# Gate and shift rows of a transformer kernel: spread by products with the identity, or by DRAM and back

## The reference, cut to what matters

```python
def ada_modulation(c, w, b):
    mod = jax.nn.silu(c) @ w + b
    return jnp.split(mod[:, None, :], 6, axis=-1)

# even layer
x = x + g_m * mix                                  # mix: two kinds of attention, then w_out
h = rms_norm(x, norm_ffn) * (1 + sc_f) + sh_f
return x + g_f * swiglu_2(h, ffn_gate, ffn_up, ffn_down)

# odd layer
x = x + g_m * (o.reshape(B, S, -1) @ w_out)        # o: sparse attention
h = rms_norm(x, norm_ffn) * (1 + sc_f) + sh_f
return x + g_f * moe_swiglu(h, router_w, router_b, exp_gate, exp_up, exp_down)
```

## Time and profile before

| | us |
|---|---|
| median of 3 runs | 2050.56 |
| lowest, highest | 2047.79, 2051.41 |
| the profiled execution | 2053.22 |
| its span, first to last instruction | 2051.3 |
| PE busy in the span | 1926.4 (94%) |
| DVE busy | 1370.7 (67%) |
| ACT busy | 1012.5 (49%) |
| POOL busy | 79.2 (4%) |

### The profile page before, as it was taken

How to read it: one execution, slowest core, us unless ns; L and a number is a source line. 1 busy time by engine, 2 the same in 40 slices (tenths; PEclk the granted TensorE clock), 3 DMA queues, 4 the chain that set the end, 5 groups by cost and what they waited for, 6 DMA issues and landing times.

```text
span 2051.3 us, 24825 instructions
## 1 busy us (share of the span) xinstructions
PE 1926.4 (94%) x9656; PEld 1614.3 (79%) x9656; DVE 1370.7 (67%) x1963; ACT 1012.5 (49%) x1372; POOL 79.2 (4%) x96
## 2 busy tenths in 40 slices
PE   8999899989998899998988999896879999999997
PEld 6888788878887778886876878795758888778886
DVE  6776776677666647676465844658574546588888
ACT  6434444454345544345445334434544435577776
POOL 1000000000000000000000100000010000000001
PEclk9999999999999999999998999998989999999998
DMA  9877477667762347775332785332075757699995
GB/s 322 267 241 235 160 250 245 226 199 247 242 233 72 111 164 232 241 245 165 84 102 82 264 296 190 122 93 93 11 265 182 246 158 250 204 351 379 379 380 211
DMA packets 270971, 432.85 MB, mean 211 GB/s; under 512 B 11075, under 2 KB 201862, under 8 KB 270598
## 3 DMA queue, kind: packets, MB, share of 16 engines
q1 hardware_dynamic: 250832, 356.65, 52.2%
q0 software_dynamic: 17968, 67.55, 9.7%
q10 hardware_dynamic: 2054, 7.06, 0.9%
HBM read 422.83 MB, written 14.68 MB: 213 GB/s over the span
## 4 chain that ended last, share of the span: by engine, by line
PE 82%; DVE 8%; ACT 6%; issue 2%; DMA 2%; ACTq 0%; DVEq 0%; SPq 0%
PE acc L2192 11%; PE acc L2194 10%; PE acc L2193 10%; PE gate_bank L2192 7%; PE gate_bank L2194 7%; PE gate_bank L2193 7%; PE up_bank L2192 7%; PE up_bank L2193 7%; PE up_bank L2194 7%; DVE w_low L1414 3%; ACT w_high L835 2%; ACT probs L950 1%; PE turn_bank L2326 1%; DMA raw<-in_e_ffn_up 1%; PE misc_bank L2261 1%
## 5 line engine op out<-in xcount | busy, mean ns | idle before, releaser
L1414 DVE TENSOR_TENSOR w_low<-raw,w_high 128x2048 fp32r<-128x2048 f32 (+2 forms) x370 | 772.7, 2099 | 299.6 <-ACT w_high L835 296.6
L835 ACT CAST w_high<-raw 128x2048 fp32r<-128x2048 f32 (+2 forms) x370 | 647.3, 1756 | 358.2 <-PE up_bank L2194 191.8
L2192 PE MATMUL gate_bank<-w_high,u_parts 128*128 128x512 f32 (+2 forms) x516 | 205.5, 398 | 14.6 <-DVE u_parts L1436 5.6
L2194 PE MATMUL gate_bank<-w_high,u_parts 128*128 128x512 f32 (+2 forms) x516 | 199.9, 387 | 0.0
L2193 PE MATMUL gate_bank<-w_low,u_parts 128*128 128x512 f32 (+2 forms) x516 | 199.9, 387 | 0.0
L2192 PE MATMUL up_bank<-w_high,u_parts 128*128 128x512 f32 (+2 forms) x500 | 194.7, 389 | 0.0
L2193 PE MATMUL up_bank<-w_low,u_parts 128*128 128x512 f32 (+2 forms) x500 | 194.3, 389 | 0.0
L2194 PE MATMUL up_bank<-w_high,u_parts 128*128 128x512 f32 (+2 forms) x500 | 194.2, 388 | 0.0
L2192 PE MATMUL acc<-w_high,hidden_high 128*128 128x512 f32 x476 | 189.5, 398 | 1.5 <-DVE w_low L1414 0.8
L2194 PE MATMUL acc<-w_high,hidden_low 128*128 128x512 f32 x476 | 186.8, 392 | 0.0
L2193 PE MATMUL acc<-w_low,hidden_high 128*128 128x512 f32 x476 | 186.2, 391 | 0.0
(11 more groups left out here) (515 smaller groups left out, 3376.5 us busy)
## 6 DMA issues: line engine op xcount, KB each, us to landing
raw<-in_o_exp_down SPq DMA_DIRECT2D x40, 1024.0 KB, 7.1
raw_ada<-in_e_ada_w POOLq DMA_DIRECT2D x24, 1024.0 KB, 5.9
raw_ada<-in_o_ada_w POOLq DMA_DIRECT2D x24, 1024.0 KB, 5.8
raw<-in_ffn_pre_wg SPq DMA_DIRECT2D x44, 512.0 KB, 5.8
raw<-in_ffn_pre_wu SPq DMA_DIRECT2D x44, 512.0 KB, 7.1
raw<-in_ffn_pre_wd SPq DMA_DIRECT2D x22, 1024.0 KB, 7.6
raw<-in_ffn_post_wg SPq DMA_DIRECT2D x44, 512.0 KB, 4.5
raw<-in_ffn_post_wu SPq DMA_DIRECT2D x44, 512.0 KB, 5.7
```

The source lines that it names most:

```text
L835: ins = nc.scalar.copy(dst(WH[c % RING]), src(RAW[RAW_SLOT[c]]))
L1414: ins = nc.vector.tensor_tensor(dst(WL[c % RING]), src(RAW[RAW_SLOT[c]]), dst(WH[c % RING]).bitcast(F32), ALU.subtract)
L2192: nc.tensor.matmul(to, sh, mh, start=first, stop=False, **kw)
L2194: return nc.tensor.matmul(to, sl, mh, start=False, stop=last, **kw)
```

## The change

Each of the six vectors is written by POOL from its eight columns to a row of a new DRAM tensor `GATES` (1024 runs of one number, `gate_out`) and read back into all 128 partitions (`gate_back`, 512 KiB). All six calls of `gate_row` on PE, ACT's copies, and their semaphores, are gone; DVE waits for `gate_in[k]` instead. Writes 0 and 1 stand in `ffn3` (after chunk 35), read 0 after chunk 37, read 1 in the even attention; writes 2 to 5 and reads 2 to 4 in `ffn4`, after chunk 47 and ahead of the late constants and the zeros; read 5 in the odd attention. The scale of the experts' norm gets a tile of its own, `ADA_LAST`, made in tile 6 of `ffn4`; `scale_of(N_OFFN)` goes.

```diff
+        ADA_LAST = sb("ada_scale_of_experts", [P, DC])
+        GATES = nc.dram_tensor("gate_rows", [6, D], F32, kind="Internal").ap()
...
+            def gate_out(k, columns):
+                pool.dma_start(GATES[k, :].rearrange("(c p) -> p c", p=P), columns, allow_slow_non_contiguous=True).then_inc(gates_out, 16)
+
+            def gate_back(k, row):
+                pool.dma_start(row, GATES[k:k + 1, :].broadcast_to([P, D])).then_inc(gate_in[k], 16)
...
             for q in range(2, ADA_DONE[3] + 1):
                 ada(q)
+                if q == ADA_DONE[2] + 3:
+                    pool.wait_ge(ada_read, 24)
+                    gate_out(0, MOD[:, 16:24])
+                    gate_out(1, MOD[:, 40:48])
+                if q == ADA_DONE[2] + 5:
+                    pool.wait_ge(gates_out, 32)
+                    pool.wait_ge(x_ready, 4 * X_POOL + 4)
+                    gate_back(0, ROWS[0][:, :])
...
+            pool.wait_ge(x_ready, 4 * X_FINAL1 + 4)
+            pool.wait_ge(at_max, GH * (G_FOX + 1))
+            gate_back(1, ROWS[1][:, :])
             for q in range(ADA_DONE[3] + 1, 48):
                 ada(q)
+            pool.wait_ge(ada_summed, 48)
+            pool.wait_ge(ada_read, 48)
+            pool.wait_ge(ada_ready, 1)
+            gate_out(2, MOD[:, 64:72])
+            gate_out(3, ADA_LAST[:, :])
+            gate_out(4, MOD[:, 72:80])
+            gate_out(5, MOD[:, 88:96])
+            pool.wait_ge(gates_out, 96)
+            pool.wait_ge(x_ready, 4 * X_EWO + 4)
+            for k, to in ((2, ROWS[0][:, :]), (3, AROW), (4, BROW)):
+                gate_back(k, to)
             pool.wait_ge(at_max, GH * (G_WIN + 2))
...
+            pool.wait_ge(x_ready, 4 * X_FFN4 + 4)
+            pool.wait_ge(at_max, GH * (G_DSA + 1))
+            gate_back(5, ROWS[1][:, :])
             pool.wait_ge(x_ready, 4 * X_OWO + 4)
             row(0, a["final_norm_2"].unsqueeze(0))
...
-            gate_row(0, X_POOL)
             blocks(b + 3, 3)
             square_sum(N_EFFN, 0)
-            gate_row(1, X_FINAL1)
             square_sum(N_EFFN, 1)
...
-            gate_row(2, X_EWO)
             prep(b + 3)
-            gathered_row(3, AROW, (GB, UB))
             square_sum(N_OFFN, 0)
-            gathered_row(4, BROW, (MB, SB))
             square_sum(N_OFFN, 1)
...
-            act.wait_ge(x_ready, 4 * X_FFN4 + 4)
-            gathered_row(5, ROWS[1], (GB, UB))
...
-                                dve.wait_ge(row_done, row + 1)
+                                dve.wait_ge(gate_in[row], 16)
...
+            def last_scale(i):
+                if i == 6:
+                    dve.wait_ge(ada_read, 48)
+                    nc.vector.scalar_tensor_tensor(ADA_LAST[:, :], MOD[:, 80:88], 1.0, vec("o_ffn"), ALU.add, ALU.mult
+                                                   ).then_inc(ada_ready, 1)
+
+            ffn(4 * FB, "ffn4", FFN_TILES, None, ada_chunk(4), last_scale)
...
-            scale_of(N_OFFN, U_OFFN, vec("o_ffn"), MOD[:, 80:88])
-            dve.sem_inc(ada_ready, 1)
...
-            dve.wait_ge(row_done, 5)
+            dve.wait_ge(gate_in[3], 16)
+            dve.wait_ge(gate_in[4], 16)
...
-            gate_row(0, MOD[:, 16:24])
             even_down(2)
             even_down(3)
-            gate_row(1, MOD[:, 40:48])
             turn_rows(N_EFFN)
-            pe.wait_ge(row_done, 2)
...
-            gate_row(2, MOD[:, 64:72])
             odd_down(2)
             odd_down(3)
-            pe.wait_ge(ada_read, 48)
-            pe.wait_ge(ada_ready, 1)
-            gate_row(3, ADA)
-            gate_row(3, MOD[:, 72:80], (MB, SB))
-            gate_row(4, MOD[:, 88:96])
             turn_rows(N_OFFN)
...
-            pe.wait_ge(row_done, 6)
```

More of the change, by code:

```diff
@@ L514, in two_blocks_kernel @@
         vec_turned, vec_ready, c_ready = sem("vec_turned"), sem("vec_ready"), sem("c_ready")
-        row_in, row_mm, row_done = sem("row_in"), sem("row_mm"), sem("row_done")
+        row_in, gates_out, gate_in = sem("row_in"), sem("gates_out"), [sem(f"gate_in{k}") for k in range(6)]
         dve_chain = sem("dve_chain")
@@ L885, in high_modulated @@
                     nc.scalar.copy(UH[:, first:first + 2, :], T[:, first:first + 2, :]).then_inc(u_hi, 2)
[L887 to L892, removed]
             def ffn(m0, name, tiles, n=None, at_tile=None):
@@ L1277, in _ @@
                     ins = nc.scalar.activation(T[:, c, :], ACC[:, c * S:(c + 1) * S], ACT.Identity,
-                                               bias=MOD[:, 72 + c:73 + c], scale=ADA[:, c:c + 1])
+                                               bias=MOD[:, 72 + c:73 + c], scale=ADA_LAST[:, c:c + 1])
                 ins.then_inc(t_act, 1)
             rows_high_part(1)
-            act.wait_ge(x_ready, 4 * X_FFN4 + 4)
-            gathered_row(5, ROWS[1], (GB, UB))
             b0 = STREAM["moe"]
@@ L1767, in scale_of @@
                 dve.wait_ge(u_hi, DC * u)
-                dve.wait_ge(ada_read, 48 if n == N_OFFN else ADA_DONE[3])
+                dve.wait_ge(ada_read, 48 if n == N_OMIX else ADA_DONE[3])
                 chain.link(nc.vector.scalar_tensor_tensor(ADA[:, :], scale, 1.0, gain, ALU.add, ALU.mult))
@@ L1861, in _ @@
             norm_modulated(N_EFFN, U_EFFN, vec("e_ffn"), MOD[:, 32:40], MOD[:, 24:32], (b + 5, b + 6))
-            ffn(4 * FB, "ffn4", FFN_TILES, None, ada_chunk(4))
+            def last_scale(i):
[4 more added lines that the diff above has]
+            ffn(4 * FB, "ffn4", FFN_TILES, None, ada_chunk(4), last_scale)
             update(A_FFN4, STREAM["ffn4"] + 3 * FB - 1, row=1)
@@ L1948, in _ @@
                 for c in (2 * cp, 2 * cp + 1):
-                    ins = nc.vector.tensor_scalar(T[:, c, :], ACC[:, c * S:(c + 1) * S], ADA[:, c:c + 1],
+                    ins = nc.vector.tensor_scalar(T[:, c, :], ACC[:, c * S:(c + 1) * S], ADA_LAST[:, c:c + 1],
                                                   MOD[:, 72 + c:73 + c], ALU.mult, ALU.add)
@@ L2068, in weighed_row @@
             def weighed_row(t):
-                dve.wait_ge(row_done, 6)
+                dve.wait_ge(gate_in[5], 16)
                 dve.wait_ge(y_second, t + 1)
@@ L2263, in modulation @@
                 mm.then_inc(ada_used, 1)
[L2265 to L2271, removed]
             def ffn(m0, name, tiles, u, chunk=lambda i: None, turned_second=None, amid_first=None):
```

## The result

| | before | after |
|---|---|---|
| median, runs | 2050.34 (5) | 2063.06 (5) |
| lowest, highest | 2046.88, 2051.41 | 2060.07, 2066.52 |
| the profiled execution, its span | 2053.22, 2051.3 | 2063.77, 2061.6 |

The account below looks back on a forecast made before the run. PE, 82% of the chain that ended last, was taken to bound the kernel. Gains of 5.2 and 7.2 us at the projections less 2.0 for the zeros gave 10.4 off 2050.6: 2040.2 us, range 2033 to 2046.5.

Parts of the forecast that it names:

- The products removed: Both output projections without row products and copies: 5.2 us gained at the even one, 7.2 at the odd one.
- Amid `ewo`: Even output projection: first row's products and a wait behind block 2 go, so block 3 starts 2.0 us earlier.
- amid `owo`: Odd output projection: the row amid it goes, 2.0 us gained; three rows behind its last product, 4.4 us.
- router: Router products behind `owo`: about half of their clock loss returns, 0.8 us gained, between 0 and 1.7.
- the clock behind `ewo`: First products of `ffn4`: PE back at full clock instead of half, 1.6 us gained, lower end 0.
- The zeros in `ffn4`: Zeros go out later in `ffn4` behind more row-read bytes, costing PE 2.0 us, 6.4 if passed on in full.
- Rival 3: Single-number writes in `ffn4` hold the DMA engines; at 0.15 us a run 19 us lost, 2059 us; chance 9%.
- a cover of 19: In `ffn4` a weight block landing in 22.12 us cost PE only 2.9, so about 19 us of delay are covered.
- the lower row: Bound chosen for a write's cost per run: `forget_weights`, 1024 runs landing in 7.0 us, at most 0.11 us each.
- One sign of being wrong: Landing times of the writes above 15 us, listed among the signs that would show the forecast wrong.
- one small DVE instruction, counted as nothing: Making the experts' scale, moved from the odd output projection to `ffn4` where DVE has room: 0 us.
- Covered: The added writes and reads on POOL's queue cost nothing: no row comes late and no engine waits.

Follow-up runs that it names:

- run 4: Changed kernel with the reads of rows 2 to 4 (1.5 MiB) moved behind `ffn4`, into the odd attention; 2064.53 us, ratio 1.0062.
- run 3: Kernel before with its late constants and zeros held back until DVE's tile 7 of `ffn4`, no writes or reads added; 2048.36 us, ratio 0.9981.
- Run 5: Changed kernel with the zeros alone moved from `ffn4` into the odd attention; 2050.81 us, ratio 0.9998.
- run 12: Changed kernel with the experts' scale kept in `silu_c`, so no tensor is added and no later one shifts; 2053.66 us, ratio 1.0008.
- run 13: Changed kernel with all writes, their reads and zeros moved to gaps behind `ffn3` and late in the odd attention, scale in `silu_c`; 2037.90 us, ratio 0.9918.
- run 7: Changed kernel with late constants and zeros ahead of the four `ffn4` writes, and those writes made twice, first to a spare tensor; 2064.63 us, ratio 1.0058.

## Why the prediction was wrong

**The products removed: right.** Amid `ewo` 1.85 us (2.0 forecast), behind it 2.4 (1.6); amid `owo` 1.5 (2.0), behind it 5.1 to the second tile's transposes (4.4), router 1.7 (0.8, upper end 1.7); 0.4 of it is lost again before the first expert product. Only the clock behind `ewo` gave nothing: 11 products in the first 4.0 us of `ffn4`, still mostly at half clock. Without it the sum was 10.8; 12.2 were measured, which earlier second tiles make up for.

**The zeros in `ffn4`: wrong in kind.** The step said that only the bytes change, 0.5 to 1.5 MiB, for 2.0 us, at most 6.4. The bytes were worth 2.7 (run 4), the late place nothing (run 3). The stage lost 12.9 us, 9.9 without the added tensor. The loss came from what stands ahead of the zeros, the writes, which stood in the sum with nothing.

**Rival 3 was the mechanism, given 9%.** It put the cost of a run at the right size (0.075 us measured, at most 0.11 by `forget_weights`), but the sum put the writes at nothing. Its own bound said otherwise: 4 x 64 x 0.11 = 28 us against a cover of 19 is a loss of 9, and I still took "the lower row" for "costs nothing". Even at 0.075 it is 19.2 us against 19. Run 5 shows 4.7 us with no zeros behind the writes. An estimate that fits: the cover of 19 us was counted from the issue of a block, so the 5 us that a block takes undisturbed (`in_e_ffn_down` 5.0 in the kernel before) are in it, and 19.2 + 5 exceeds it by 5. And the cover, spent once, isn't there for the zeros: together 16.7 us above an undisturbed `ffn4` (212.9 - 196.2). Rival 3 should have asked for the sum of the two stops, not for r alone. One sign of being wrong that the prediction named came: the writes took up to 19.0 us to land, more than 15.

**The added tensor: missing.** Its cost was never considered; "one small DVE instruction, counted as nothing" looked at the instruction, not at where its result lies. It costs 6 to 11 us by the ratios and 6.4 by the starts of the products, more than half of the net gain that was forecast. Without it the change would be within the noise (run 12).

**Covered: mostly right.** Writes 0 and 1 and read 0 in `ffn3` cost nothing (201.25 in run 12, 201.24 in run 13 without them), no row came late, and DVE waited for none.

**The balance.** 12.2 gained; 9.9 lost in `ffn4` against the kernel before (212.9 against 203.0); 6 to 11 by the address: 4 to 9 us slower, against a measured 11 with an interval of 7 to 15. In the two profiles the 10.3 us of span are 3.5 up to the end of `ffn3`, -1.4 in the even attention and `ewo`, 12.8 in `ffn4`, -6.4 from there to the first expert product and 1.7 in the experts (rounded). What is left is about what one profile says of a stage: `ffn4` takes 200.2 to 204.0 in four profiles of the kernel before and its copies with unused bytes, and the odd attention's first part, up to its heads, 78.6 to 81.7 with the same instructions, by the clock. The start of `ffn3` lies between 764 and 775 us from run to run as well. That remainder isn't assigned. Run 13 comes out better: 12.2 gained, 5.4 in `ffn4` (197.6 against 203.0), 0.9 lost in the odd attention's heads make 16.7 us, measured 0.82%, 16.8.

## What to carry to other kernels

Count the runs of a transfer, not its bytes: here a transposing write of single numbers took 0.075 us a number per engine, and the weight stream beside it fell to 28 GB/s. So give it longer runs, or a place where no weight is due, and see that bulk transfers behind it have such a place too. Stops that follow each other draw on one store of loaded weights; add them up before comparing with what is covered. And when a kernel bound by TensorE gets a new tensor, look whether weights and streamed data still lie alike modulo 64: put it last, or make it a multiple of 64 bytes. `v_high` of this kernel doesn't lie so; moving it alone would be worth about 2 us by the starts, and wasn't tried.

## What the runs showed of the hardware

- Single-number writes to DRAM, 4096 in 16 engines: 19.2 us (run 7 against the changed kernel). Beside them 4 KiB packets of another queue took 1.1 to 3.0 us in place of 0.165, and 28 GB/s passed in 15 us. The same bytes in runs of 32 landed in 4.2 us (median) in place of 14.3.
- A product of 128x128 weights with fp32 data took in `ffn3` 227 ns from start to start with both at the same address modulo 64, and 233 with 32 bytes between them, for `w_low,hidden_high`; 389 and 395 ns in the rows. `v_high`, 32 bytes off from the weights, took 396, and 392 when it lay as they do. Over this kernel the 32 bytes made 0.3 to 0.5%.
